# Expert 0's sample rows selected already transposed, in the two routed layers of a diffusion backbone

## What is computed

```python
def ec_moe(x, router_w, w_gate, w_up, w_down):
    bsz, n_tok, _ = x.shape
    cap = n_tok * EC_CAPACITY // N_EXPERTS
    aff = jax.nn.softmax(jnp.einsum('btd,de->bte', x, router_w).astype(jnp.float32), axis=-1)
    gate, idx = lax.top_k(jnp.swapaxes(aff, 1, 2), cap)
    bidx = jnp.arange(bsz)[:, None, None]
    xe = x[bidx, idx]
    hid = jax.nn.silu(jnp.einsum('becd,edf->becf', xe, w_gate)) * jnp.einsum('becd,edf->becf', xe, w_up)
    ye = jnp.einsum('becf,efd->becd', hid, w_down) * gate[..., None].astype(x.dtype)
    return jnp.zeros_like(x).at[bidx, idx].add(ye)
```

## Time and profile before

| | us |
|---|---|
| median of 3 runs | 1415.14 |
| lowest and highest run | 1413.36, 1418.28 |
| the profiled execution, first to last instruction (its span) | 1413.9 |

### The profile page before, as it was taken

The page is one execution under the profiler, slowest core; times in us unless marked ns, Lnnn a source line. Parts: engine busy times, 40 slices in busy tenths (PEclk is TensorE's granted clock), DMA queues, the critical chain, the costliest instruction groups (busy, mean ns, idle before and its releaser), DMA issues. The chain is left out here.

```text
span 1413.9 us, 27268 instructions
## 1 busy us (share of the span) xinstructions
PE 1331.0 (94%) x11153; PEld 815.3 (58%) x11153; DVE 697.4 (49%) x1634; ACT 528.6 (37%) x1221; POOL 280.4 (20%) x239
## 2 busy tenths in 40 slices
PE   5999998889899999999998999989899999999996
PEld 1755666766686444444448999555588444444443
DVE  1536614677635343334346646956654433334436
ACT  2723113666423222222226468665532322222213
POOL 0001103586002011111110030655301101111101
PEclk8999999999999999999998999999999999999997
DMA  9688961041526999999982012050043999999995
GB/s 364 237 328 304 350 217 27 23 158 34 194 107 257 369 377 375 374 378 373 387 307 74 1 64 68 1 223 1 1 183 125 374 368 378 378 377 381 376 350 180
DMA packets 105800, 333.82 MB, mean 236 GB/s; under 512 B 23182, under 2 KB 29164, under 8 KB 99532
## 3 DMA queue, kind: packets, MB, share of 16 engines
q1 hardware_dynamic: 99276, 310.11, 57.9%
q0 software_dynamic: 5824, 19.86, 5.9%
q10 hardware_dynamic: 576, 2.10, 0.4%
HBM read 308.13 MB, written 23.89 MB: 235 GB/s over the span
## 5 line engine op out<-in xcount | busy, mean ns | idle before, releaser
L1961 PE MATMUL psum<-wraw,proj 128*32 128x512 f32 x3072 | 399.6, 594 | 2.7 <-ACT proj L2071 1.2
L1967 PE MATMUL psum<-wraw,proj 128*16 128x256 f32 x3072 | 234.1, 379 | 0.6 <-ACT proj L2076 0.6
L1967 PEld LDWEIGHTS psum<-wraw,proj 128*16 128x16 f32 x3072 | 89.8, 97 | 229.5 <-issue 224.6
L1961 PEld LDWEIGHTS psum<-wraw,proj 128*32 128x32 f32 x3072 | 96.2, 110 | 74.1 <-issue 8.5
L1927 POOL DMA_INDIRECT x_rows<-modrow,idx x30 | 42.8, 1427 | 452.7 <-DVE modrow L2176 452.7
L2089 ACT ACTIVATE proj<-psum 128x320 f32<-128x320 f32 x32 | 14.0, 437 | 286.0 <-PE psum L2027 286.0
L2138 DVE TENSOR_SCALAR proj<-psum,proj 128x64 f32<-128x64 f32 x232 | 55.7, 313 | 106.5 <-PE psum L1949 106.5
L1336 POOL TENSOR_SCALAR ring<-ring,small 128x640 f32<-128x640 f32 x48 | 90.2, 1883 | 40.6 <-DVE small L1275 40.1
L2171 DVE SCALAR_TENSOR_TENSOR modrow<-psum,proj 64x512 f32<-64x512 f32 x60 | 44.9, 749 | 84.3 <-PE psum L1967 83.9
L2163 DVE TENSOR_TENSOR proj<-proj,psum 64x512 f32<-64x512 f32 x32 | 22.1, 690 | 128.1 <-ACT proj L2096 128.1
L1266 DVE TENSOR_REDUCE small<-psum 128x1 f32<-128x640 f32 (+1 forms) x80 | 57.3, 717 | 53.2 <-PE psum L1241 52.8
(11 more groups left out here) (520 smaller groups left out, 2437.6 us busy)
## 6 DMA issues: line engine op xcount, KB each, us to landing
wraw<-in_exp_w_gate_dram SPq DMA_DIRECT2D x128, 512.0 KB
wraw<-in_exp_w_up_dram SPq DMA_DIRECT2D x128, 512.0 KB
wraw<-in_exp_w_down_dram SPq DMA_DIRECT2D x128, 512.0 KB
ring<-in_ada_w_dram SPq DMA_DIRECT2D x29, 1024.0 KB, 6.5
hold<-in_ada_w_dram SPq DMA_DIRECT2D x14, 1024.0 KB, 6.6
ring<-in_ev_w_in_dram SPq DMA_DIRECT2D x4, 2048.0 KB, 12.3
xr<-x_rows SPq DMA_DIRECT2D x15, 512.0 KB, 7.4
proj<-in_ada_w_dram SPq DMA_DIRECT2D x5, 1024.0 KB, 9.0
```

Source lines behind the costliest of these rows:

```text
L1961: mm = pe.matmul(psum[quad(q, 32), b, :], xs[:, quad(q % 2, 32)], pair[q // 2], start=first, stop=last)
L1967: mm = pe.matmul(psum[quad(q, CAPP), b, 0:QP], xs[:, CAPS:CAP], pair[q // 2][:, q % 2 * QP:(q % 2 + 1) * QP], start=first, stop=last)
```

## The change

For expert 0's samples the operands of the selection change places: for each tile t and each k of the order 0, 4, 1, 5, 2, 6, 3, 7 the strided slice `xr[:, t, k::KD]` (128 tokens by 128 channels) is stationary and `pick[:, t, :]` (64 columns) moves. The product is then the transposed piece k, 128 channels by 64 places: pieces 0, 4, 1, 5 lie in PSUM bank 0, pieces 2, 6, 3, 7 in bank 1. The copy to `picked_s`, the four transposes and the five `keep_busy` matmuls behind the selection are gone. Each bank's last matmul increments the semaphore, which is now `xT`; ACT starts at 1 (bank 0 complete), DVE and SP's load 8 at 2 (both complete).

```diff
@@ out_and_route
             def sync_after(sp, selected):
...
-                sp.wait_ge(selected, 1)
+                sp.wait_ge(selected, 2)
                 load_weights(sp, l, 8, ready)
...
+            FIRST_ROWS = (0, 4, 1, 5, 2, 6, 3, 7)
...
                 for t in range(ST):
                     pe.wait_ge(s["pick"], t + 1)
-                    for c in range(2):
-                        mm = pe.matmul(psum[64 * c:64 * c + CAPS, 1, :], pick[:, t, :], columns(t, 4 * c, 4 * c + 4), start=(t == 0), stop=(t == ST - 1))
+                    for n, k in enumerate(FIRST_ROWS):
+                        mm = pe.matmul(bank(n // 4)[:, n % 4 * CAPS:(n % 4 + 1) * CAPS], xr[:, t, k::KD], pick[:, t, :], start=(t == 0 and n % 4 == 0), stop=(t == ST - 1),
+                                       skip_group_check=True)
+                        if t == ST - 1 and n % 4 == 3:
+                            mm.then_inc(selected, 1)
                     if t == ST - 2:
                         turn_affinities(pe, 1)
-                mm.then_inc(selected, 1)
-                keep_busy(pe, 5, 5)
@@ experts
-                routed["sync_after"](sp, s["sel"])
+                routed["sync_after"](sp, s["xT"])
...
                 def first_hidden():
-                    pe.wait_ge(s["selc"], 1)
-                    for k in range(4):
-                        mm = pe.transpose(bank(k // 2)[:, k % 2 * P:(k % 2 + 1) * P], picked_s[:, k, :], ident[:, :])
-                    mm.then_inc(s["xT"], 2)
...
                         if n == 7:
-                            pe.wait_ge(s["selc"], 2)
+                            pe.wait_ge(s["selc"], 1)
...
-                routed["tensor_choice"](pe, s["sel"])
+                routed["tensor_choice"](pe, s["xT"])
...
                 def modulate_picked(k):
-                    return act.activation(xgT[:, 0, k, 0:CAPS], bank(0)[:, k % 4 * P + k // 4 * CAPS:k % 4 * P + (k // 4 + 1) * CAPS], ACT.Identity,
+                    at = CAPS * (2 * (k % 4) + k // 4)
+                    return act.activation(xgT[:, 0, k, 0:CAPS], bank(0)[:, at:at + CAPS], ACT.Identity,
                                           scale=scale_of[:, 0, k:k + 1], bias=shift_of[:, 0, k:k + 1])
...
-                act.wait_ge(s["sel"], 1)
-                act.activation(picked_s, bank(1).rearrange("p (k d) -> p k d", k=4), ACT.Copy).then_inc(s["selc"], 1)
-                act.wait_ge(s["xT"], 2)
+                act.wait_ge(s["xT"], 1)
                 for k in (0, 4, 1):
                     modulate_picked(k).then_inc(s["xk"], 1)
                 modulate_picked(5).then_inc(s["xca"], 1)
-                act.wait_ge(s["sel"], 2)
+                act.wait_ge(s["sel"], 1)
```

More of the change, by code:

```diff
@@ L1881, in experts @@
             xgT, hidT = cs(2, KD, CAP), cs(FB, CAP)
-            picked_s, picked_p = sg[:, 0:512].rearrange("p (k d) -> p k d", k=4), hid[:, 0:256].rearrange("p (k d) -> p k d", k=2)
+            picked_p = hid[:, 0:256].rearrange("p (k d) -> p k d", k=2)
             assert cs.at <= EXPERT_TOP
@@ L2142, in modulate_picked @@
                 def modulate_picked(k):
-                    return dve.tensor_scalar(xgT[:, 0, k, 0:CAPS], bank(1)[:, (k % 4 - 2) * P + k // 4 * CAPS:(k % 4 - 2) * P + (k // 4 + 1) * CAPS], scale_of[:, 0, k:k + 1], shift_of[:, 0, k:k + 1],
+                    at = CAPS * (2 * (k % 4 - 2) + k // 4)
+                    return dve.tensor_scalar(xgT[:, 0, k, 0:CAPS], bank(1)[:, at:at + CAPS], scale_of[:, 0, k:k + 1], shift_of[:, 0, k:k + 1],
                                              ALU.mult, ALU.add)
```

## The result

| | before | after |
|---|---|---|
| median, us | 1414.25 (4 runs, 1412.92 to 1418.28) | 1431.67 (4 runs, 1427.66 to 1434.85) |
| ratio, 95% interval | 1 | 1.0107 (1.0083 to 1.0131) |
| profiled span, us | 1413.9 | 1429.5 |
| mean granted clock | 0.982 | 0.967 |

The change makes the kernel slower: by 17.4 us by the difference of the medians, by 15.1 us by the ratio (11.7 to 18.5), and by 15.6 us by the profiled spans. The forecast was hardly any difference, 1414.7, and the range ended at 1418.2. The prediction was wrong, and of its rivals B, at 1425.9, is nearest.

The account below looks back on a forecast made before the run. The prediction took the weight loads to bound the kernel, with PE already touching that wall: 2.17 us earlier a layer would gain 0 in the first and 0.4 in the second, so 1415.14 - 0.4 = 1414.7 us, range 1411.5 to 1418.2.

Parts of the forecast that it names:

- rival B: Selection: strided stationary slices load at half speed, 0.245 us each, PE 5.67 us late a layer, 1425.9 us; chance 0.07.
- The failed step: Selection: each of 64 instructions with a strided stationary slice was priced at 0.1225 us, 7.84 us in all.
- the sum: Selection to first product: the selection ends at 452.85, so PE is ready 2.17 us earlier in each layer.
- Rival D: Expert loop: waits of 1 to 2 us near its end could halve PE's clock, at worst 6.8 us, 1421; chance 0.02.
- the wall: Expert loop: weight loads are slower than PE by 1.4 us an expert, so PE's lead becomes waits for up matrices.
- ACT's part: Behind the selection: ACT's first modulation is over by 452.6, before PE can begin the product at 452.85.
- The room left in the second layer: Second layer's expert loop: loads leave PE 0.4 us to gain, with ends of 0 and 2.17.
- Load 8: SP's queue: this weight load waits until both banks are complete, 0.24 us later than before, at no cost.
- Rival A: Expert loop: no wall in most runs, so PE keeps its lead, 2 x 2.17 us, 1410.8; chance 0.10.
- Rival C: Selection: load and matmul don't overlap, 0.06 us more for each of 64, PE 1.7 us late a layer, 1417.9; chance 0.05.

Follow-up runs that it names:

- e3_wide: The changed kernel, strides kept, with each selection matrix read twice so that 128 columns move: median 1424.92 us, ratio 1.0060 to the kernel before.
- e1_bench: The kernel before with 20 filler matmuls replaced by groups of eight float32 matmuls or transposes at several strides: 0.108 us an instruction contiguous, 0.234 at stride 8.
- e4: The kernel before without the copy, transposes and filler behind the selection: median 1416.90 us, ratio 0.9998.
- e5: The kernel before without copy, transposes and filler, and with the up load of expert 7 cut to an eighth: median 1410.74 us, ratio 0.9960.
- e6: The kernel before with only the up load of expert 7 cut to an eighth: median 1417.54 us, ratio 1.0000.
- e2_contig: The changed kernel with contiguous stationary slices, so expert 0's samples get other channels: median 1421.82 us, ratio 1.0041 to the kernel before.
- e7_contig_wide: The changed kernel with contiguous stationary slices and 128 moving columns: median 1414.27 us, ratio 1.0003 to the kernel before.
- e8_bench2: The kernel before with test groups between 48 filler instructions, at the upper clock: stride 8 matmuls 0.235 us apart, transposes 0.111, 48 contiguous with 64 columns 0.111.

## Why the prediction was wrong

**The failed step** is the one that says: "The stationary slice is strided by eight; so is that of L1949 ... I take 0.1225". Measured: 0.239 in the changed kernel, 0.234 and 0.235 in the two benches. The stand-in was a transpose, one instruction each, and a transpose isn't slowed by its stride (0.106 and 0.111); a float32 matmul, two instructions each, is. Why is not shown. I had written down both differences, 80 rows and a transpose, under rival B, and gave B 0.07 all the same. The rows turned out to be of no account, the operation decided. In the sum, 64 x 0.1225 = 7.84 should have been 64 x 0.239 = 15.3, and PE is 5.3 and 5.1 us late instead of 2.17 early.

**Rival B** had 0.245 a load, 5.67 us a layer and 2 x 5.67 - 0.54 = 10.8 in all. Its mechanism alone, e3_wide, gave 0.241 ((459.65 - 448.09) / 48), a first product 5.35 and 5.17 us late, and 9.8 in all. It was right to a tenth. The row that spoke for it, moving operands at double cost, was the better guide: e1_bench has 0.232 for a moving and 0.234 for a stationary slice. As to the Trainium skill, SBUF — State Buffer, section Door 1: The DMA port swizzle, by which a float32 stride of eight isn't free: I had written that the trace disagrees for stationary operands. That was wrong for matmuls and stays true for transposes. Its bound differs, too: by that page of the Trainium skill a stride of up to four is free, and the benches show 2 free (0.114), 3 at 0.171 and 4 at 0.229, nearly the full double.

**A term that no case had**: PE's clock was down through the selection, in both layers, and slowed the first products by 1.4 and 1.9 us. Rival D had looked for it in the loop, behind waits, and from 463.2 and 1131.3 on the kernel's loops kept the upper clock. By the profiles, both layers of each kernel:

| | 64 columns move | 128 columns move | 512 columns move (before's selection) |
|---|---|---|---|
| stride 8 | 17.1 and 20.5 us (the change) | 3.4 and 3.4 us, at no cost (e3_wide) | before none; e4 3.4 and 3.4; e5 none; e6 none and 3.4 |
| contiguous | 13.7 and 20.5 us (e2_contig) | none (e7_contig_wide) | |

Two things come apart. Whether the clock falls doesn't depend on the new selection: where it fell, it did so between 1.3 us ahead of the selection's start and 1.4 us behind it, with either form. What PE does just before the selection is the same in all of them (the logits' L1456, the spreading matmul, two filler ones). What brings the fall on, and why some layers have none, is open. So e7's none against e3's 3.4 can't be laid to the stride: before's own selection shows both. How long it stays down does go with the moving width: 13.7 to 20.5 us in all four layers with 64 columns, never over 3.4 with 128 or 512 (the two benches, which have before's selection, show 3.4 there in both layers, too). The mean clocks of all runs agree for the strided pair: 0.963 to 0.969 in the changed kernel's four, 0.977 to 0.985 in e3_wide's six. PE had no gap in the four new versions, and the clock fell in three of them and stayed down in two all the same. In e8_bench2 48 such instructions with 64 columns amid dense matmuls kept the upper clock; what decides in general is open.

**Right** were: the wall, its place (up matrices of experts 12 to 15) and its price, shown by e7_contig_wide with 2.9 and 2.4 us of waits where 2 to 3 and 1 to 2 were named (PE was 2.76 us ahead there and not 2.17), and by e4 against e5; and that ACT's part needs no time of its own. The room left in the second layer, 0.4 us in the sum, was 1.26 in e4 and nothing in e7. Load 8 was named 0.24 us later at no cost. It was issued at 459.40, 4.4 us later than before (455.02), because the selection took so long, and still no product waited for it:

```profile
459.40 1.75 SPq L1404 DMA_DIRECT2D wraw<-in_exp_w_gate_dram  x4
```

**Rival A**, no wall, is refuted by the same runs: it would have given e7_contig_wide 2 x 2.76 = 5.5 us, and that has 0. **Rival C**, load and matmul one after the other, is refuted by the spacing: 0.108 with 64 moving columns (e1_bench) and 0.114 with 128 (e7). One after the other, the 64 columns more would have added 0.06 by the prediction's own figure.

**The sum again**, with measured terms: 5.3 + 5.1 for the selection, 1.4 + 1.9 for the clock, -0.75 for the waits that a late PE no longer meets, make 12.95. The spell around 940 and the earlier start of this one run add 3.5 - 1.0. The split between stride and clock is not the only one: against before, the last down products come 9.8 us later in all with the stride alone (e3_wide), 9.7 with the low clock alone (e2_contig), and 13.0, not 19.5, with both (the change: 289.06 and 289.36 after the selection's start). A strided load takes no notice of the clock, so the two overlap. No version was looked for that gives the contiguous slices the right channels, by another layout of expert 0's weights: by e7_contig_wide, it would meet the wall and end where the kernel before does.

## What to carry to other kernels

Price a strided operand by rows of the same operation in the same role: a transpose says nothing of a float32 matmul, and where only the wrong stand-in exists, the chance belongs with the doubled price, since 64 instructions turn 0.12 us into a whole verdict. When work on PE gets shorter in front of a loop that its loads bound, first ask how much later the last load may come; here it was nothing in one layer and at most 1.3 us in the other, with 1.74 and 2.76 us saved ahead. And a stretch of many small matmuls needs its granted clock read along with its spacing, because one cost can cover the other.

## What the runs showed that I had not expected

- A float32 matmul's stationary slice: strides of 1, 2, 3, 4 and 8 elements load in 0.108, 0.114, 0.171, 0.229 and 0.234 us an instruction. Rows (80 or 128) and clock (0.231 at the lower, 0.235 at the upper) don't matter. A contiguous load does follow the clock: 0.108 to 0.111 us at the upper, 0.215 at the lower.
- A transpose with a stride of 8 loads in 0.106 to 0.111 us at the upper clock.
- In a row of selecting matmuls with 64 moving columns, PE busy all the time, the clock stayed at 1.2 GHz for 17.1 us (445.2 to 462.2) in the first layer and 20.5 us (1110.8 to 1131.2) in the second. With 128 or 512 moving columns at the same place it was back at 2.4 GHz after 3.4 us or did not fall.
- The two costs are not a sum: 9.8 us for the stride, 9.7 for the low clock, 13.0 for both.
